# Eleven up units of an MLP by seven half-size products instead of eight

## Chip, cores and metric

The kernel runs on one core of a Trainium2 chip. The metric is the device time of one execution in microseconds (us); a change is judged by medians of runs. All arithmetic is on float32 data.

## What is computed

The reference is a transformer block of width 1024 on 512 rows, followed by a second stack of two layers (pooling, attention, gated convolution FFNs). The change concerns the MLP of the first block alone:

```
m = rms_norm(h, mlp_norm[i])                       # h: 512 x 1024
h = h + jnp.square(jax.nn.relu(m @ w_mlp_up[i])) @ w_mlp_down[i]   # up: 1024 x 4096, down: 4096 x 1024
```

## The kernel before

Activations are held transposed: 8 blocks of 128 channels on the partitions by 512 rows. A product of two float32 matrices is made of three TensorE products, because each operand is split into a high part (rounded to the multiplier's float32r format) and a low part (the rest): high x high, high x low, low x high. AH and AL are the parts of the activations, WH and WL those of the weights, HH and HL those of the squared hidden values.

The weights are cut into units of 128 x 2048 floats, listed in PLAN. A unit `up i` gives the hidden tiles m = 2i and 2i+1, each 128 hidden channels by 512 rows: 2 tiles x 8 channel blocks x 3 = 48 matmuls of 128x128 by 128x512 into one PSUM bank a tile. A unit `down i` is as large; groups of four down units consume eight hidden tiles and add their result to X. The order in the MLP is up 0 to 4, down 0 to 3, up 5 to 8, down 4 to 7, up 9 to 12, down 8 to 11, up 13 to 15, down 12 to 15. Before, the order is written in `mlp_order` and all engines walk through the same list.

Each engine runs its own program in order and waits on semaphores. SP loads a unit into one of two RAW buffers once the low part of the unit two before is made (`load`, L2457). ACT copies RAW to the high part in one of three WH slots (`split`, L1287), when PE is done with what the slot held; DVE subtracts to get the low part WL (`split`, L1677). A hidden tile goes: DVE takes relu and scale from PSUM (L2156, mark "up"), ACT squares (L1516) and rounds (L1519, mark "hh"), DVE makes HL (L2158, mark "hl"). DVE adds a down result to X (L1707). PE's triples of a tile are at L585 to L587, and those with the weights moving (the pooling stage: 256 columns) at L591 to L593. Six PSUM banks and a seventh are taken in a ring; the eighth holds norm sums. POOL issues a few DMAs during the MLP (`ev`, `pe_x`).

Of the kernel before, what the change touches and what calls it, by code (L numbers as in the profile page):

```python
# [15 lines left out]
P = 128  # L16
# [154 lines left out]
def memory(nc, ctx):  # L171
# [14 lines left out]
    k.WH = [a.tile(f"WH{i}", [P, UE], R) for i in range(NW)]  # L186
    wl_at = a.at
    k.WL = [a.tile(f"WL{i}", [P, UE], R) for i in range(NW)]
    k.rb = a.tile("rb", [P, S])
    k.sq = [a.tile(f"sq{i}", [P, S]) for i in range(2)]  # L190
    dg_at = a.at
    k.dg = a.tile("dg", [P, 4, P])
# [64 lines left out]
    k.pH = a.tile("pH", [P, 2, S], R)  # L257
    k.pL = a.tile("pL", [P, 2, S], R)
    k.pj = a.tile("pj", [P, 8, S])
    rel_at = a.at  # L260
    k.rel = a.tile("rel", [16, 513])
    k.ev = a.tile("ev", [16, 640])
# [64 lines left out]
    return (k.WH[j][:, 0:n].rearrange("p (k n) -> p k n", k=kc), k.WL[j][:, 0:n].rearrange("p (k n) -> p k n", k=kc))  # L327


def arrived(k, name):  # L330
    return k.arrived[name], 16


def mlp_order():

    for g in range(5):
        for i in range(4 * g, 4 * g + 1) if g < 4 else ():
            yield from up_order(i)
        if g > 0:
            for i in range(4):  # L340
                yield "split", UNIT["down", 4 * (g - 1) + i] + 2
                yield "down", g - 1, 2 * i
                yield "down", g - 1, 2 * i + 1
        for i in range(4 * g + 1, 4 * g + 4) if g < 4 else ():
            yield from up_order(i)
# [221 lines left out]
def tensor_program(k, e):  # L567
# [426 lines left out]
    def down(name, g, n, base, kc, m):  # L994

        u = UNIT[name, 4 * g + m // 2]
        a, l = split_view(k, u, kc)
        b = next_bank(7)
        cols = slice(m % 2 * P, m % 2 * P + P)
        w.wait_ge(WLO(u), *free[b])  # L1000
        for c in range(kc):
            s = (base + c) % NH
            w.wait_ge(DVE("hl", name, base + c))
            t = triple(bank[b][:, :], a[:, c, cols], l[:, c, cols], k.HH[s][:, :], k.HL[s][:, :], c == 0, c == kc - 1)
        t.then_inc(*in_bank(b, "res", n, m))
        free[b] = [DVE("x", n, m)]
        if m % 2:
            MM.also("unit", u)

    opened = {}  # L1010
    for step, *x in mlp_order():
        if step == "open":
            w.wait_ge(WLO(UNIT["up", 0]))
            bs = [next_bank(7), next_bank(7)]
            w.wait_ge(*free[bs[0]], *free[bs[1]])
            for c in TILES[:7]:
                w.wait_ge(DVE("al", 1, c))
                for i in range(2):
                    product(UNIT["up", 0], 8, i, bs[i], ks=[c], ends=(TILES[0], TILES[7]))
        elif step == "close":  # L1020
            m, = x
            w.wait_ge(DVE("al", 1, TILES[7]))
            product(UNIT["up", 0], 8, m, bs[m], ks=TILES[7:], ends=(TILES[0], TILES[7])).then_inc(*in_bank(bs[m], "up", m))
            free[bs[m]] = [DVE("up", m)]
            MM.also("unit", UNIT["up", 0])
        elif step == "tile":
            m, = x
            b = next_bank(7)
            w.wait_ge(WLO(UNIT["up", m // 2]), *free[b])
            product(UNIT["up", m // 2], 8, m % 2, b).then_inc(*in_bank(b, "up", m))  # L1030
            free[b] = [DVE("up", m)]
            MM.also("unit", UNIT["up", m // 2])
        elif step == "sums":
            norm_sums(1, DVE("acc", 1, 7))
        elif step == "spread":
            norm_spread(1)
        elif step == "down":
            g, m = x
            down("down", g, 2 + g, 8 * g, 8, m)

# [232 lines left out]
def scalar_program(k, e):  # L1273
# [4 lines left out]
    def split(u, *also):  # L1278

        if u >= len(PLAN):  # L1280
            return
        n = PLAN[u][2]
        w.wait_ge(loaded(k, u), *also)
        before = [v for v in range(u) if SLOT_OF[v] == SLOT_OF[u]]
        if before:
            w.wait_ge(MM("unit", before[-1]))
# [207 lines left out]

    w.wait_ge(arrived(k, "pe"))
    e.activation(k.pH[:, :, :], k.pe_x[:, :, :], AF.Copy).then_inc(*ACT.mark("pH"))

    def free_high(name, m, n0, group_of):  # L1500

        if m >= NH:
# [2 lines left out]
    for step, *x in mlp_order():  # L1505
        if step == "split":
            split(*x)
        elif step == "spread":
            spread_rows(1)
        elif step == "rest":  # L1510
            m, = x
            i = m % 2
            w.wait_ge(DVE("up", m))
            if m > 1:
                w.wait_ge(DVE("hl", "down", m - 2))
            e.activation(t2s[i][:, :], k.t1s[i][:, 0:S], AF.Square).then_inc(*ACT.mark("usq", m))  # L1516
            w.wait_ge(ACT("usq", m))
            free_high("down", m, 2, lambda m: m // 8)
            e.activation(k.HH[m % NH][:, :], t2s[i][:, :], AF.Copy).then_inc(*ACT.mark("hh", "down", m))  # L1519
        elif step == "down":  # L1520
# [143 lines left out]
def vector_program(k, e):  # L1664
# [462 lines left out]

    w.wait_ge(ACT("pH"))  # L2130
    e.tensor_tensor(k.pL[:, :, :], k.pe_x[:, :, :], k.pH[:, :, :].bitcast(F), SUB).then_inc(*DVE.mark("pL"))
# [5 lines left out]
    def parts(n, gcol, c, used):  # L2137

        w.wait_ge(DVE("x", k.x_of[n], c), used)
        e.tensor_scalar(AH[:, c, :], X[:, c, :], gain(gcol, c), None, MUL).then_inc(*DVE.mark("ah", n, c))  # L2140
        low_part(n, gcol, c, DVE("ah", n, c))

    for step, *x in mlp_order():
        if step == "split":
            split(*x)
        elif step == "sums":
            mean_square(1)
        elif step == "spread":
            spread_rows(1)
        elif step == "rest":  # L2150
            m, = x
            i, s = m % 2, m % NH
            w.wait_ge(MM("up", m), ACT("rb", 1))
            if m > 1:
                w.wait_ge(ACT("usq", m - 2))
            e.scalar_tensor_tensor(k.t1s[i][:, 0:S], bank[where["up", m]][:, :], 0.0, rb[:, :], MAX, MUL).then_inc(*DVE.mark("up", m))  # L2156
            w.wait_ge(ACT("hh", "down", m))
            e.tensor_tensor(k.HL[s][:, :], t2s[i][:, :], k.HH[s][:, :].bitcast(F), SUB).then_inc(*DVE.mark("hl", "down", m))  # L2158
        elif step == "down":
# [199 lines left out]
def pool_program(k, e):  # L2359
# [40 lines left out]


    w.wait_ge(DVE("al", 1, 3), MM("res", 16, 3))
    e.dma_start(k.pe_x[:, :, :], k.PT).then_inc(k.arrived["pe"], 16)
    e.dma_start(k.rel[:, :], k.REL).then_inc(k.arrived["rel"], 16)
    root(1)
    w.wait_ge(DVE("ev"))
    for i in range(16):
        w.wait_ge(MM("up", 2 * i))
        e.dma_start(k.EV.ap()[i:i + 1], k.ev[i:i + 1, None, :].to_broadcast([1, 64, 640])).then_inc(k.arrived["ev"], 16)
    w.wait_ge((k.arrived["ev"], 256))  # L2410
    e.dma_start(k.BC[:, :, :, :], k.BND).then_inc(k.arrived["band"], 16)
    root(2)
# [229 lines left out]
```

## Time and profile before

| | |
|---|---|
| median of 3 runs | 1646.34 us (1645.31 to 1647.6) |
| span of the profiled execution | 1644.3 us |
| PE busy | 1638.7 us, 8084 matmuls |
| PE weight loads busy | 1336.2 us, 8084 |
| DVE busy | 939.2 us, 1385 instructions |
| ACT busy | 615.9 us, 828 instructions |

The profiled execution's own time is its span; outside the span lie some 2 us up to the median of the runs. The page's engines: PE is TensorE, DVE is VectorE, ACT is ScalarE, SP and POOL issue DMAs. Matmuls overlap by their latencies, so their pace is read from starts, not from lengths.

### The profile page before, as it was taken

To read this page: it belongs to the slowest core of one execution; us is meant where nothing else is said; L and a number is where in the kernel's file an instruction comes from. 1 tells how busy PE (TensorE), PEld (TensorE's weight loads), DVE (VectorE), ACT (ScalarE), POOL (GpSimd) and SP (SyncE) were. 2 spreads that over 40 slices of the span, in tenths; PEclk is the share of its full clock that TensorE was granted. 3 is DMA by queue.
4 is the path that set the end of the run, shared out by engine and by line. 5 is a ranking of instruction groups with operands and counts; after the bars stand their busy time and mean duration, and the time that the engine had idled before them with its cause. 6 is when DMAs were issued, how large, how long until landed. Compare 5 with 4: busy or idle time off the path is not lost.

```text
span 1644.3 us, 19097 instructions
## 1 busy us (share of the span) xinstructions
PE 1638.7 (100%) x8084; PEld 1336.2 (81%) x8084; DVE 939.2 (57%) x1385; ACT 615.9 (37%) x828; POOL 84.6 (5%) x80
## 2 busy tenths in 40 slices
PE   9999999999999999999999999999999999999999
PEld 7877878888888888888888888877777888888887
DVE  6797665444333547577466457555655576366353
ACT  5576344322332346433222223355565333122121
POOL 1300000000000000000000000311201100000000
PEclk9999999999999999999999999999999999999999
DMA  5310227454454421223322223323221223222311
GB/s 187 116 36 27 103 93 128 120 89 130 87 111 85 135 88 52 77 103 107 124 83 96 103 83 100 123 78 101 77 76 52 77 103 104 102 102 94 110 59 71
DMA packets 28054, 155.94 MB, mean 95 GB/s; under 512 B 3712, under 2 KB 5392, under 8 KB 12096
## 3 DMA queue, kind: packets, MB, share of 16 engines
q1 hardware_dynamic: 26352, 149.75, 25.6%
q0 software_dynamic: 1328, 4.86, 5.0%
q8 instruction: 64, 1.05, 0.3%
q14 instruction: 22, 0.18, 0.0%
q10 hardware_dynamic: 288, 0.10, 0.0%
HBM read 149.98 MB, written 4.72 MB: 94 GB/s over the span
## 4 chain that ended last, share of the span: by engine, by line
PE 98%; ACT 1%; DVE 1%; POOL 0%; DMA 0%; issue 0%; SPq 0%; DVEq 0%
PE bank L585 26%; PE bank L587 26%; PE bank L586 26%; PE bank L591 3%; PE bank L593 3%; PE bank L592 3%; PE bank L1216 1%; PE bank L840 1%; PE bank L1226 1%; PE bank L1242 1%; PE bank L825 1%; PE bank L865 1%; PE bank L850 1%; PE bank L769 0%; PE bank L1102 0%; PE bank L1204 0%
## 5 line engine op out<-in xcount | busy, mean ns | idle before, releaser
L585 PE MATMUL bank<-AH,WH 128*128 128x512 f32 (+1 forms) x1150 | 451.4, 393 | 0.2 <-DVE X L1707 0.2
L587 PE MATMUL bank<-AH,WL 128*128 128x512 f32 (+1 forms) x1150 | 447.8, 389 | 0.0
L586 PE MATMUL bank<-AL,WH 128*128 128x512 f32 (+1 forms) x1150 | 447.6, 389 | 0.0
L1677 DVE TENSOR_TENSOR WL<-RAW,WH 128x2048 fp32r<-128x2048 f32 (+1 forms) x133 | 298.5, 2247 | 190.7 <-ACT WH L1287 190.7
L1287 ACT ACTIVATE WH<-RAW 128x2048 fp32r<-128x2048 f32 (+1 forms) x133 | 248.3, 1871 | 260.1 <-PE bank L587 240.3
L585 PEld LDWEIGHTS bank<-AH,WH 128*128 128x128 f32 (+1 forms) x1150 | 215.5, 187 | 48.0 <-issue 2.6
L587 PEld LDWEIGHTS bank<-AH,WL 128*128 128x128 f32 (+1 forms) x1150 | 215.5, 187 | 45.8
L586 PEld LDWEIGHTS bank<-AL,WH 128*128 128x128 f32 (+1 forms) x1150 | 215.6, 187 | 45.6 <-issue 1.0
L585 PE MATMUL bank<-HH,WH 128*128 128x512 f32 x608 | 239.6, 394 | 0.0
L587 PE MATMUL bank<-HH,WL 128*128 128x512 f32 x608 | 238.4, 392 | 0.0
L586 PE MATMUL bank<-HL,WH 128*128 128x512 f32 x608 | 236.0, 388 | 0.0
L1707 DVE TENSOR_TENSOR X<-X,bank 128x512 f32<-128x512 f32 x111 | 76.0, 685 | 192.2 <-PE bank L587 192.1
L587 PEld LDWEIGHTS bank<-HH,WL 128*128 128x128 f32 x608 | 114.1, 188 | 26.8
L586 PEld LDWEIGHTS bank<-HL,WH 128*128 128x128 f32 x608 | 114.1, 188 | 25.5
L585 PEld LDWEIGHTS bank<-HH,WH 128*128 128x128 f32 x608 | 114.3, 188 | 22.8
L1596 ACT ACTIVATE t2s<-t2s,par 128x512 f32<-128x512 f32 x44 | 31.9, 724 | 186.8 <-DVE t2s L2261 186.8
L591 PE MATMUL bank<-WH,AH 128*128 128x512 f32 x224 | 90.0, 402 | 0.0
L593 PE MATMUL bank<-WH,AL 128*128 128x512 f32 x224 | 87.5, 391 | 0.0
L592 PE MATMUL bank<-WL,AH 128*128 128x512 f32 x224 | 87.3, 390 | 0.0
L1601 ACT ACTIVATE HH<-cvs 128x512 fp32r<-128x512 f32 x44 | 27.8, 632 | 126.0 <-DVE cvs L2267 126.0
L1516 ACT ACTIVATE t2s<-t1s 128x512 f32<-128x512 f32 x32 | 20.2, 632 | 97.4 <-DVE t1s L2156 97.4
L1294 ACT ACTIVATE sq<-X 128x512 f32<-128x512 f32 x49 | 30.9, 630 | 65.6 <-DVE X L1707 61.6
(306 smaller groups left out, 1732.9 us busy)
## 6 DMA issues: line engine op xcount, KB each, us to landing
RAW<-in_W SPq DMA_DIRECT2D x124, 1024.0 KB, 4.8
RAW<-in_W SPq DMA_DIRECT2D x9, 768.0 KB, 4.1
X<-in_XT SPq DMA_DIRECT2D x16, 256.0 KB, 5.5
ev_scratch<-ev POOLq DMA_DIRECT2D x16, 160.0 KB, 7.5
Gb<-ev_scratch SPq DMA_DIRECT2D x16, 128.0 KB, 2.9
Gb<-ev_scratch SPq DMA_DIRECT2D x16, 112.0 KB, 2.7
out<-X SPq DMA_DIRECT2D x7, 256.0 KB, 2.0
RAW<-in_W SPq DMA_DIRECT2D x2, 512.0 KB, 5.4
```

Of the source, the lines that this page charges most:

```text
L585: e.matmul(o, a, h, start=first, stop=False)
L586: e.matmul(o, a, l, start=False, stop=False)
L587: return e.matmul(o, c, h, start=False, stop=last)
L591: e.matmul(o, h, a, start=first, stop=False)
L592: e.matmul(o, h, c, start=False, stop=False)
L593: return e.matmul(o, l, a, start=False, stop=last)
L1287: e.activation(k.WH[SLOT_OF[u]][:, 0:n], k.RAW[RAW_OF[u]][:, 0:n], AF.Copy).then_inc(*WHI.mark(u))
L1294: e.activation(k.acc if j == 0 else sq[(j - 1) % 2][:, :], src, AF.Square).then_inc(*ACT.mark("sqr", n, j))
L1596: e.activation(t2s[i][:, :], t2s[i][:, :], AF.Silu, bias=par[:, PC_CB + 22 * l + m:PC_CB + 22 * l + m + 1]).then_inc(*ACT.mark("silu", l, m))
L1601: e.activation(k.HH[m % NH][:, :], k.cvs[i][:, :], AF.Copy).then_inc(*ACT.mark("hh", name, m))
L1677: e.tensor_tensor(k.WL[j][:, 0:n], k.RAW[RAW_OF[u]][:, 0:n], k.WH[j][:, 0:n].bitcast(F), SUB).then_inc(*WLO.mark(u))
L1707: e.tensor_tensor(X[:, m, :], X[:, m, :], src, ADD).then_inc(*DVE.mark("x", n, m))
```

## The change

Up units 5 to 15 (`FAST`) are computed as a 2 x 2 block product with seven products of half-size blocks in place of eight: a, c, b, f, d, g, e (`FORMS`), each 4 channel blocks x 3 parts = 12 matmuls of 128x128 by 128x256, that is 84 matmuls a unit in place of 48. The inputs are sums of blocks. Of the activations these are made once, during down 0 to 3 (`shapes`, tiles TH and TL). Of the weights, three sums S1, S2, S3 are made for each fast unit in `stage`, and S4 is written over a block of RAW (`added`); four plus three quarter pieces are then split. WH and WL become rings of 12 quarter pieces; a fast unit takes 7, a plain one 4. The outputs need seven additions of blocks (`first_row`, `second_row`, `y`). The order inside a turn (one unit's time on PE) is written out in `turn_order`. The ACT and DVE work of hidden tiles moves into the steps "one", "two" and "low". The load of `pe_x` and its split move from before the MLP to down 13. The diff, cut:

```diff
+FIRST_FAST = 5
+FAST = {UNIT["up", i] for i in range(FIRST_FAST, 16)}
+FORMS = "acbfdge"
+def turn_of(u):
+    held = max((name[1] for name in held_until(u, 0, 4)), default=-1)
+    return min(max(held + 1, u - 2), u - 1)
+def turn_order(u):
+    _, i, _ = PLAN[u]
+    fast = u in FAST
+    if u - 1 in FAST:
+        yield "two", u - 1
+    for v in (u + 1, u + 2):
+        if turn_of(v) == u:
+            if v not in FAST:
+                yield "split", v
+            else:
+                if turn_of(v) == v - 2:
+                    yield "add", v
+                yield "raw", v
+    if fast:
+        yield "mid", u
+    if u - 1 in FAST:
+        yield "low", 2 * PLAN[u - 1][1] + 1
+    if u + 1 in FAST:
+        yield "stage", u + 1
+    if u + 2 in FAST and turn_of(u + 2) == u + 1:
+        yield "add", u + 2
+    if fast:
+        yield "one", u
+        yield "low", 2 * i
+    else:
+        if i < 3:
+            for c in ((0, 1), (2,), (3,))[i]:
+                yield "shapes", c
+        yield "down", i // 4, 2 * (i % 4)
+        yield "down", i // 4, 2 * (i % 4) + 1
+        if i == 13:
+            yield "pe",
 PE
+    def fast_products(u):            # step "mid"
+        bs = [next_bank(7) for _ in range(3)]
+        w.wait_ge(WLO(u), *free[bs[0]])
+        w.wait_ge(*(DVE("tl", c) for c in range(4)))
+        form_product(u, "a", bank[bs[0]])
+        w.wait_ge(WLO("stage", u))
+        form_product(u, "c", bank[bs[0]])
...
+        form_product(u, "g", bank[bs[2]])
+        w.wait_ge(DVE("y", u))
+        form_product(u, "e", bank[bs[0]])
 ACT
+        elif step == "raw":
+            w.wait_ge(loaded(k, u), DVE("s4", u), *(MM(*name) for name in held_until(u, 0, 4)))
+            for h, _, cols in ring_views(k, u, 0, 4):
+                t = e.activation(h, k.RAW[RAW_OF[u]][:, cols], AF.Copy)
+        elif step == "stage":
+            w.wait_ge(DVE("s2", u), *(MM(*name) for name in held_until(u, 4, 3)))
+        elif step == "mid":
+            w.wait_ge(MM("form", u, "c"), DVE("z", before) if before else DVE("t4", 3))
+            e.activation(k.G[:, 0:256], bank[k.where["fast", u][0]][:, 0:256], AF.Copy).then_inc(*ACT.mark("q1", u))
+        elif step in ("one", "two"):
+            w.wait_ge(DVE("up", m), DVE("hl", "down", m - 2))
+            e.activation(t2s[i][:, :], k.t1s[i][:, 0:S], AF.Square).then_inc(*ACT.mark("usq", m))
+            e.activation(k.HH[m % NH][:, :], t2s[i][:, :], AF.Copy).then_inc(*ACT.mark("hh", "down", m))
 DVE
+    def added(u):                    # step "add"
+        w.wait_ge(loaded(k, u), MM("spread", 1), *([WLO("stage", before)] if before else []))
+        e.tensor_tensor(k.stage[:, 0:2, :], raw[:, 0:4:3, :], raw[:, 2:3, :].to_broadcast([P, 2, QUARTER]), ADD)   # s1
+        e.tensor_tensor(k.stage[:, 2, :], raw[:, 0, :], k.stage[:, 1, :], ADD)      # waits s1, marks s2
+        e.tensor_tensor(raw[:, 2, :], raw[:, 1, :], k.stage[:, 2, :], ADD)          # waits s2, marks s4
+    def first_row(u):                # step "one"
+        w.wait_ge(MM("form", u, "g"), DVE("y", u))
+        e.tensor_tensor(k.G[:, 256:512], k.YZ[:, 0, :], bank[b[2]][:, 256:512], ADD)    # t
+        e.tensor_tensor(k.t1s[0][:, 0:S], k.G[:, :], bank[b[1]][:, :], ADD)             # row, waits t
+        e.scalar_tensor_tensor(k.t1s[0][:, 0:S], k.t1s[0][:, 0:S], 0.0, rb[:, :], MAX, MUL)   # up, waits row
+    def second_row(u):               # step "two": z (waits form e), row, up, likewise
+        elif step == "raw":
+            w.wait_ge(WHI(u))        # then WL = RAW - WH, 2048 columns, marks WLO(u)
+        elif step == "stage":
+            w.wait_ge(WHI("stage", u))   # then 1536 columns, marks WLO("stage", u)
+        elif step == "mid":
+            w.wait_ge(ACT("q1", u))
+            e.tensor_tensor(k.YZ[:, 0, :], k.G[:, 0:256], bank[...][:, 256:512], ADD).then_inc(*DVE.mark("y", u))
+        elif step == "low":
+            w.wait_ge(ACT("hh", "down", m))
+            e.tensor_tensor(k.HL[m % NH][:, :], t2s[m % 2][:, :], k.HH[m % NH][:, :].bitcast(F), SUB)
```

In a turn of a fast unit u between two others the list of steps is thus: two u-1, raw u+1, mid u, low (odd tile of u-1), stage u+1, add u+2, one u, low (even tile of u). Every engine takes its part of each step in this order.

## Rows read from the trace of the kernel before

**Rows 1.** The page, its first line and the chain that ended last, by engine.
```profile
span 1644.3 us, 19097 instructions
...
PE 98%; ACT 1%; DVE 1%; POOL 0%; DMA 0%; issue 0%; SPq 0%; DVEq 0%
```

**Rows 2.** Three stretches of the MLP: us, busy time (instructions) of each engine.
```profile
432.00:465.00 33.00, 33.00 (x148) 27.31 (x147) 14.91 (x15) 12.75 (x16) 1.51 (x3) 1.00 0.67 97
465.00:476.00 11.00, 11.00 (x50) 9.04 (x49) 4.96 (x5) 3.64 (x4) 0.00 (x0) 1.00 0.57 112
476.00:520.00 44.00, 44.00 (x194) 36.14 (x193) 14.80 (x13) 8.94 (x6) 0.50 (x1) 1.00 0.29 111
```

**Rows 3.** Timeline of PE, products of 512 columns: start, length (us).
```profile
344.82 0.39 PE L586 MATMUL bank<-AL,WH 128*128 128x512 f32 x1
...
351.85 0.39 PE L587 MATMUL bank<-AH,WL 128*128 128x512 f32 x1
```

**Rows 4.** Timeline of PE, products of 256 columns, in two stretches.
```profile
645.20 0.28 PE L591 MATMUL bank<-WH,HH 128*128 128x256 f32 x1
...
652.15 0.28 PE L593 MATMUL bank<-WH,HL 128*128 128x256 f32 x1
...
654.08 0.28 PE L591 MATMUL bank<-WH,HH 128*128 128x256 f32 x1
...
657.71 0.28 PE L593 MATMUL bank<-WH,HL 128*128 128x256 f32 x1
```

**Rows 5.** Weight loads of the 256-column products, grouped: busy us, mean ns.
```profile
L591 PEld LDWEIGHTS bank<-WH,HH 128*128 128x128 f32 x32 | 6.0, 188 | 0.0
```

**Rows 6.** Timeline of DVE, one up unit of the MLP.
```profile
450.47 2.29 DVE L1677 TENSOR_TENSOR WL<-RAW,WH 128x2048 fp32r<-128x2048 f32 x1 [1.12 <-ACT WH L1287]
452.68 0.68 DVE L2156 SCALAR_TENSOR_TENSOR t1s<-bank,rb 128x512 f32<-128x512 f32 x1
454.73 0.69 DVE L2158 TENSOR_TENSOR HL<-t2s,HH 128x512 fp32r<-128x512 f32 x1 [1.36 <-ACT HH L1519]
457.49 0.69 DVE L2156 SCALAR_TENSOR_TENSOR t1s<-bank,rb 128x512 f32<-128x512 f32 x1 [2.07 <-PE bank L587]
459.54 0.69 DVE L2158 TENSOR_TENSOR HL<-t2s,HH 128x512 fp32r<-128x512 f32 x1 [1.36 <-ACT HH L1519]
461.35 2.29 DVE L1677 TENSOR_TENSOR WL<-RAW,WH 128x2048 fp32r<-128x2048 f32 x1 [1.12 <-ACT WH L1287]
```

**Rows 7.** Timeline of DVE, two neighbouring down units.
```profile
317.30 2.29 DVE L1677 TENSOR_TENSOR WL<-RAW,WH 128x2048 fp32r<-128x2048 f32 x1 [1.32 <-ACT WH L1287]
...
328.29 2.29 DVE L1677 TENSOR_TENSOR WL<-RAW,WH 128x2048 fp32r<-128x2048 f32 x1 [1.32 <-ACT WH L1287]
```

**Rows 8.** Timeline of ACT, same up unit.
```profile
447.33 0.63 ACT L1516 ACTIVATE t2s<-t1s 128x512 f32<-128x512 f32 x1 [3.52 <-DVE t1s L2156]
448.00 0.63 ACT L1519 ACTIVATE HH<-t2s 128x512 fp32r<-128x512 f32 x1
448.53 1.91 ACT L1287 ACTIVATE WH<-RAW 128x2048 fp32r<-128x2048 f32 x1
```

**Rows 9.** DVE by line and shape, 240 to 264 us: busy us, mean ns.
```profile
L2131 DVE TENSOR_TENSOR pL<-pe_x,pH 128x1024 fp32r<-128x1024 f32 x1 | 1.2, 1225 | 2.0 <-ACT pH L1498 2.0
...
L1689 DVE TENSOR_SCALAR m<-bank 128x4 f32<-128x4 f32 x1 | 0.1, 143 | 0.0
```

**Rows 10.** Timeline of DVE, an addition and what reads its result.
```profile
551.09 0.68 DVE L1707 TENSOR_TENSOR X<-X,bank 128x512 f32<-128x512 f32 x1
551.80 0.49 DVE L2140 TENSOR_SCALAR AH<-X,par 128x512 fp32r<-128x512 f32 x1
```

**Rows 11.** The page, loads of weights: KB each, us from issue to landing.
```profile
RAW<-in_W SPq DMA_DIRECT2D x124, 1024.0 KB, 4.8
```

**Rows 12.** Timeline of PE, start of the execution.
```profile
1.06 4.21 PE L658 MATMUL bank<-rb 128*128 128x128 f32 x18 [1.06 <-DVE rb L1729]
...
7.80 0.40 PE L585 MATMUL bank<-AH,WH 128*64 128x512 f32 x1
```

More of the change, by code:

```diff
@@ L334, in mlp_order @@
 def mlp_order():
[L336 to L345, printed above, removed]
+    for i in range(FIRST_FAST):
+        yield from up_order(i)
+    for u in range(UNIT["down", 0], UNIT["down", 15] + 1):
+        yield from turn_order(u)
+def turn_order(u):
[22 more added lines that the diff above has]
+        yield "low", 2 * i
+    else:
+        if i < 3:
[5 more added lines that the diff above has]
+            yield "pe",
 def up_order(i):
@@ L1008, in down, with form_product @@
             MM.also("unit", u)
+    left, right = slice(0, 256), slice(256, 512)
+    moving = {"a": (AH, AL, 0, left), "b": (AH, AL, 4, left), "f": (AH, AL, 4, right), "g": (AH, AL, 0, right)}
+    half_bank = {"a": (0, left), "c": (0, right), "b": (1, left), "f": (1, right), "g": (2, left), "d": (2, right), "e": (0, right)}
+    def form_product(u, x, b):
+        place = places(u)[FORM_OF[x]] * QUARTER
+        n, cols = half_bank[x]
+        for c in range(4):
+            a, l = (z[:, place + c * P:place + c * P + P] for z in (k.WHR, k.WLR))
+            if x in moving:
+                zh, zl, c0, half = moving[x]
+                h, lo = zh[:, c0 + c, half], zl[:, c0 + c, half]
+            else:
+                h, lo = (z[:, c, "dce".index(x), :] for z in (k.TH, k.TL))
+            e.matmul(b[:, cols], a, h, start=c == 0 and x in "abd", stop=False, skip_group_check=True)
+            e.matmul(b[:, cols], a, lo, start=False, stop=False, skip_group_check=True)
+            t = e.matmul(b[:, cols], l, h, start=False, stop=c == 3, skip_group_check=True)
+        t.then_inc(*MM.mark("form", u, x))
+    def fast_products(u):
+        m = 2 * PLAN[u][1]
+        bs = [next_bank(7) for _ in range(3)]
+        k.where["fast", u] = bs
+        w.wait_ge(WLO(u), *free[bs[0]])
[3 more added lines that the diff above has]
+        form_product(u, "c", bank[bs[0]])
+        w.wait_ge(*free[bs[1]])
+        form_product(u, "b", bank[bs[1]])
+        form_product(u, "f", bank[bs[1]])
+        w.wait_ge(*free[bs[2]])
+        form_product(u, "d", bank[bs[2]])
+        form_product(u, "g", bank[bs[2]])
+        w.wait_ge(DVE("y", u))
+        form_product(u, "e", bank[bs[0]])
+        for name in (("up", m), ("up", m + 1), ("unit", u)):
+            MM.also(*name)
+        free[bs[0]], free[bs[1]], free[bs[2]] = [DVE("z", u)], [DVE("row", m)], [DVE("row", m + 1)]
     opened = {}
@@ new lines, in added @@
+    def added(u):
+        raw = k.RAW[RAW_OF[u]][:, :].rearrange("p (c n) -> p c n", c=4)
+        before = max((v for v in FAST if v < u), default=0)
+        w.wait_ge(loaded(k, u), MM("spread", 1), *([WLO("stage", before)] if before else []))
+        e.tensor_tensor(k.stage[:, 0:2, :], raw[:, 0:4:3, :], raw[:, 2:3, :].to_broadcast([P, 2, QUARTER]), ADD).then_inc(
+            *DVE.mark("s1", u))
+        w.wait_ge(DVE("s1", u))
+        e.tensor_tensor(k.stage[:, 2, :], raw[:, 0, :], k.stage[:, 1, :], ADD).then_inc(*DVE.mark("s2", u))
+        w.wait_ge(DVE("s2", u))
+        e.tensor_tensor(raw[:, 2, :], raw[:, 1, :], k.stage[:, 2, :], ADD).then_inc(*DVE.mark("s4", u))
@@ new lines, in first_row @@
+    def first_row(u):
+        m, b = 2 * PLAN[u][1], where["fast", u]
+        w.wait_ge(MM("form", u, "g"), DVE("y", u))
+        e.tensor_tensor(k.G[:, 256:512], k.YZ[:, 0, :], bank[b[2]][:, 256:512], ADD).then_inc(*DVE.mark("t", u))
+        w.wait_ge(DVE("t", u), ACT("usq", m - 2))
+        e.tensor_tensor(k.t1s[0][:, 0:S], k.G[:, :], bank[b[1]][:, :], ADD).then_inc(*DVE.mark("row", m))
+        w.wait_ge(DVE("row", m))
+        e.scalar_tensor_tensor(k.t1s[0][:, 0:S], k.t1s[0][:, 0:S], 0.0, rb[:, :], MAX, MUL).then_inc(*DVE.mark("up", m))
@@ L2158, in vector_program @@
             e.tensor_tensor(k.HL[s][:, :], t2s[i][:, :], k.HH[s][:, :].bitcast(F), SUB).then_inc(*DVE.mark("hl", "down", m))
+        elif step == "shapes":
+            shapes(*x)
+        elif step == "add":
+            added(*x)
+        elif step == "raw":
+            u, = x
+            w.wait_ge(WHI(u))
+            for h, l, cols in ring_views(k, u, 0, 4):
+                t = e.tensor_tensor(l, k.RAW[RAW_OF[u]][:, cols], h.bitcast(F), SUB)
+            t.then_inc(*WLO.mark(u))
+        elif step == "stage":
+            u, = x
+            w.wait_ge(WHI("stage", u))
+            for h, l, cols in ring_views(k, u, 4, 3):
+                t = e.tensor_tensor(l, k.stage[:, :, :].rearrange("p i n -> p (i n)")[:, cols], h.bitcast(F), SUB)
+            t.then_inc(*WLO.mark("stage", u))
+        elif step == "mid":
+            u, = x
+            w.wait_ge(ACT("q1", u))
+            e.tensor_tensor(k.YZ[:, 0, :], k.G[:, 0:256], bank[where["fast", u][0]][:, 256:512], ADD).then_inc(*DVE.mark("y", u))
+        elif step == "one":
+            first_row(*x)
+        elif step == "two":
+            second_row(*x)
+        elif step == "low":
+            m, = x
+            w.wait_ge(ACT("hh", "down", m))
+            e.tensor_tensor(k.HL[m % NH][:, :], t2s[m % 2][:, :], k.HH[m % NH][:, :].bitcast(F), SUB).then_inc(*DVE.mark("hl", "down", m))
+        elif step == "pe":
+            w.wait_ge(ACT("pH"))
+            e.tensor_tensor(k.pL[:, :, :], k.pe_x[:, :, :], k.pH[:, :, :].bitcast(F), SUB).then_inc(*DVE.mark("pL"))
         elif step == "down":
```

117 lines of the change are left out of this document (108 added, 9 removed).

## Prediction

> **What bounds the kernel now.** I read the chain that ended last first: it lies on PE for 98% of a span of 1644.3 us [rows 1]. So every matmul removed from the MLP is worth its pace, if what feeds PE keeps up. Next, the stretches by engine: in 33 us of three up units DVE is busy 14.9 and ACT 12.8, in 44 us of four down units 14.8 and 8.9 [rows 2]. The reader is to see that both have about half of their time free, and that this is a mean over a simple pattern. Last, the timelines, for paces and hand-overs. The pace of PE is the distance of starts: 512-column products start 7.03 us apart over 31 intervals, 0.2268 us each [rows 3]. An up unit (48) is 10.88 us, which is also the distance of DVE's splits there, 450.47 to 461.35 [rows 6]; a down unit takes 10.99 [rows 7].
>
> **What PE gains.** Products of 256 columns stand in the trace: 59 intervals of 0.1178 us and 32 of 0.1134 [rows 4]. The second is half of 0.2268 to the digit. I take 0.1134: a fast unit is 84 x 0.1134 = 9.53 us in place of 10.88, 11 units give 11 x 1.35 = -14.9 us (by 0.1178: 9.90 and -10.8). A bound from above is the weight load, 188 ns long [rows 5]; loads of neighbouring products overlap in rows 4, or these could not start 0.113 apart.
>
> The Trainium skill (TensorE: Matmul & The Clock Gate, Back-to-back issue gap) gives 81 ns for 128 columns and 131 for 512 in a sustained stream, so half the columns would cost much more than half. By a line between its figures (an estimate) 256 columns take about 98 ns and a fast unit 8.2 us against 6.3 for 48 full ones, 1.9 us more; rows 3 and 4 do not agree with either figure, and the measured paces decide.
>
> **What the change adds on DVE and ACT.** DVE lengths: 0.69 us for 512 columns, 1.225 for 1024, 2.29 for 2048 [rows 6, 9], a straight line of 0.267 us a 256 columns. So 256 columns take 0.42 and 1536 take 1.76. The 256-column price is not in the trace; its bounds are 0.14 (4 columns) and 0.69 [rows 6, 9], and I take the line because three points lie on it. The next instruction starts 0.08 before the end of one that it does not depend on (450.47 to 452.68 for 2.29), and 0.03 after the end of one that it does [rows 6, 10]. ACT: 0.63 for 512, 1.91 for 2048 [rows 8], 0.03 more to hand over, 0.54 to the next independent one.
>
> Now one whole turn between two fast units, from one step `y` to the next, in DVE's order, which is fixed:
> - y 0.34, low 0.61, low parts of the stage 1.68, its end 0.11: 2.7.
> - add: s1 on 1024 columns 1.25, s2 0.72, s4 0.61: 2.6.
> - first row: t 0.45, row 0.72, up 0.72: 1.9. Then DVE can only wait: the next step, low, needs ACT's square 0.66 and rounding 0.66: 1.3. low itself 0.6.
> - second row: 1.9. Then `raw` waits on ACT, whose list has square 0.66, rounding 0.54 and only then the high parts of 2048 columns 1.94: 3.1. Low parts of raw 2.2. Then y.
>
> Sum 16.4 us (16.7 where a unit wraps the ring and its split is two instructions), 10.9 of it busy. PE has 9.53 us of work in it. The last product of a unit, e, waits for y, and the next unit's products stand behind e in PE's queue; so PE stops before e, 6.9 to 7.1 us a full turn. A turn without add (the fourth unit of a group; the third of the last) is 13.8: stop 4.2 to 4.3. In a group's first fast unit y starts 4.35 us after its first product (c at 2.7, ACT, raw), while e is due at 8.2: no stop. Its loop to the second unit is 17.2 (the stage waits for product b), of which 9.5 is work and 3.4 the slack just named: 4.3. The same additions for the last group, where one add lies elsewhere, give 4.1.
>
> Stops before e: 4.3 + 7.1 + 4.2, 4.3 + 6.9 + 4.2, 4.1 + 4.3 = 39.4 us.
>
> **One more wait, at down 12.** Its first accumulation needs hidden tile 31 in its eighth block. From y of unit up 15 DVE and ACT need: y and low 0.95, first row 1.9, ACT 1.3, low 0.6, second row 1.9, ACT square, rounding and the split of down 13 3.1, then DVE's splits of down 13 and down 14, 4.4, which stand ahead of low(31) in the list, and low 0.7: 15.0. PE: 0.46 to y's end, e 1.36, 21 products 4.8: 6.6. Stop 8.4. In the other groups the first down unit reads tiles finished long before: nothing.
>
> **Edits that I cost at nothing.** shapes: a column block is 8 DVE instructions, 3.9 us, and about 1 of waiting on ACT, four times 20 us, within 44 us of down units in which DVE is busy 14.8 [rows 2]; with two adds and a stage (2.6 twice and 1.8) that is 42. The last TL is made 5.5 us before up 5 needs it, the stage of up 5 4 us before product c. Without this cover up 5 starts later by what is missing. Additions to X wait longer, but seven banks give them more than two down units. Loads: a RAW buffer is freed with the low parts of raw and filled 4.8 us later [rows 11], while its reader is at least 5 us behind. The load of `pe_x` goes behind the last `ev` issue on POOL's queue and is read a down unit or more later. The split of `pe_x` was off PE's path before, so moving it gives nothing.
>
> **The clock.** At the start of the execution 18 small products take 4.21 us, and the first product of 0.40 us stands at 7.80 [rows 12]; the products between are longer. After a pause, then, PE may work at the lower of its two levels for up to 6.7 us, which costs half of that, 3.4. Before e this is paid out of the stops themselves (9.5 + 3.4 is less than 13.8). Only after the 8.4 us stop nothing covers it: 0 to 3.4, I take 2.
>
> **Sum.** 1644.3 - 14.9 + 39.4 + 8.4 + 2 = 1679.2 against the profiled span; the median of the runs is 2.0 above that span: **1681 us**.
>
> **Rivals.**
> 1. VectorE keeps up. For: it is half idle [rows 2]. Against: 10.9 us of its own work a full turn against 9.5. The mechanism would be that the steps between y and y overlap the hand-overs, so that only the work counts. Then there are two stops of 1.4 and the last of perhaps 6: -14.9 + 9 gives 1640; with none at all, 1631. It decides from where the stops together fall below 14.9 us, 1.7 each over nine in place of 5.3. Chance 0.05, a little of it within 0.2% of before.
> 2. Half-size products do not cost half: PE would wait for weight loads. At 0.188 us [rows 5] a fast unit is 15.8 us, 11 x 4.9 = +54, and of the stops only the last, 7, is left: 1707. Against: rows 4. Chance 0.02. The skill's rule on issue gaps, above, points this way.
> 3. The clock stays low through the runs of fast units, since PE pauses in each. At 0.2268 us for 256 columns a unit is 19.0 us, longer than VectorE's loop: 11 x 8.1 + 7 = +96: 1742 at the end, and anything between for a part. For: every turn has a pause of 4 to 7 us, which the trace of before never has behind its start. Against: the clock came up within 6.7 us of work, and a unit is 9.5. Chance 0.08. The Trainium skill (TensorE: Matmul & The Clock Gate, Why this matters for your kernels) warns that idle gaps between bursts send the clock back to the lower level; no run so far shows this within a kernel.
>
> The forecast has 0.85.
>
> **Range.** The 256-column price, three a loop, at 0.14 or 0.69 moves nine loops by 0.8 each, 8 us either way; hand-overs of 0.02 to 0.08 in place of 0.03 move the total by -3 to +8; PE's pace hardly moves it, since the fast runs go by VectorE; the clock 0 to 3.4, or more in rival 3. Together 1667 to 1700. What a measurement of this kernel can tell from no change is about 0.2%, 3 us: faster 0.05, same 0.02, slower 0.93.
>
> **What would show it.** Starts of y 16 to 17.5 us apart inside a group and 13.8 at its end; a PE timeline with idle time before product e released by DVE YZ, 40 us in sum, and 8 us before the last block of down 12's first tile, released by HL; DVE near 11 of 16.5 us busy; the ACT copy of RAW waiting on nothing but its place in the queue. 256-column products at 0.113 to 0.118 apart. I am wrong if e does not wait, if idle time stands elsewhere (before product a or c: splits late; before the first down product: loads), or if the pace inside a burst is 0.227.

## The result and the profile after

The median is 1686.03 us (1684.21 to 1688.71, 4 runs) against 1646.03 us (1645.31 to 1647.6) before: ratio 1.0236, 95% interval 1.0223 to 1.025, slower by 40 us. The forecast was 1681 us, in a range of 1667 to 1700. The profiled execution spans 1683.7 us, 39.4 us more than before. Its page, first line and chain by engine, to be read against [rows 1]:

```profile
span 1683.7 us, 20082 instructions
...
PE 70%; DVE 7%; ACT 3%; issue 1%; POOL 0%; DVEq 0%; ACTq 0%
```

The chain was followed back from the end to 320 us only, so its shares add to 81% of the span. VectorE and ScalarE, which had 1% each before, now have 10% together. Two stretches of the MLP, the first group of fast units and the down units behind it, columns as in [rows 2] and then the granted clock:

```profile
338.00:393.00 55.00, 45.82 (x337) 45.16 (x337) 39.65 (x50) 20.28 (x25) 1.51 (x3) 0.88 0.46 70
393.00:437.80 44.80, 44.80 (x194) 36.31 (x193) 24.10 (x25) 11.46 (x9) 0.50 (x1) 1.00 0.41 118
```

In 55 us of four fast units VectorE is busy 39.7 us, three quarters of the time, and PE 45.8; the granted clock is 0.88 on average. In the down units VectorE has time left. What PE waited for in the MLP (us in total, times, longest):

```profile
PE bank L1134 <- DVE YZ L2415: 23.3, 8, 6.1
PE bank L694 <- DVE HL L2423: 7.9, 1, 7.9
```

L1134 is the first product of each triple of a fast unit, and its waits stand before e; the one at L694 stands before the first down product that reads hidden tile 31. These are the two waits of the forecast, 31.2 us together. VectorE between the y of unit up 6 and that of up 7, to be read against [rows 6]:

```profile
360.74 0.41 DVE L2415 TENSOR_TENSOR YZ<-G,bank 128x256 f32<-128x256 f32 x1
361.07 0.68 DVE L2423 TENSOR_TENSOR HL<-t2s,HH 128x512 fp32r<-128x512 f32 x1
361.68 1.75 DVE L2410 TENSOR_TENSOR WLR<-stage,WHR 128x1536 fp32r<-128x1536 f32 x1
363.53 1.23 DVE L2352 TENSOR_TENSOR stage<-RAW 128x1024 f32<-128x1024 f32 x1
364.79 0.69 DVE L2355 TENSOR_TENSOR stage<-RAW,stage 128x512 f32<-128x512 f32 x1
365.52 0.69 DVE L2357 TENSOR_TENSOR RAW<-RAW,stage 128x512 f32<-128x512 f32 x1
366.13 0.42 DVE L2363 TENSOR_TENSOR G<-YZ,bank 128x256 f32<-128x256 f32 x1
366.58 0.69 DVE L2365 TENSOR_TENSOR t1s<-G,bank 128x512 f32<-128x512 f32 x1
367.30 0.69 DVE L2367 SCALAR_TENSOR_TENSOR t1s<-t1s,rb 128x512 f32<-128x512 f32 x1
369.35 0.69 DVE L2423 TENSOR_TENSOR HL<-t2s,HH 128x512 fp32r<-128x512 f32 x1 [1.36 <-ACT HH L1699]
369.96 0.41 DVE L2373 TENSOR_TENSOR YZ<-G,bank 128x256 f32<-128x256 f32 x1
370.41 0.69 DVE L2375 TENSOR_TENSOR t1s<-YZ,bank 128x512 f32<-128x512 f32 x1
371.13 0.69 DVE L2378 SCALAR_TENSOR_TENSOR t1s<-t1s,rb 128x512 f32<-128x512 f32 x1
375.07 2.36 DVE L2404 TENSOR_TENSOR WLR<-RAW,WHR 128x1536 fp32r<-128x1536 f32 x2 [3.25 <-ACT WHR L1679]
377.35 0.41 DVE L2415 TENSOR_TENSOR YZ<-G,bank 128x256 f32<-128x256 f32 x1
```

From y to y are 16.61 us (forecast 16.4 to 16.7). L2410 is the stage's low part, L2352 to L2357 the add, L2363 to L2367 the first row, L2423 the low parts of hidden tiles, L2373 to L2378 the second row, L2404 raw. Two gaps are to be seen: 1.36 us before the low part at 369.35, and 3.25 before the split at 375.07. What ScalarE did in the second, to be read against [rows 8]:

```profile
371.86 0.63 ACT L1696 ACTIVATE t2s<-t1s 128x512 f32<-128x512 f32 x1 [2.53 <-DVE t1s L2378]
372.52 0.63 ACT L1699 ACTIVATE HH<-t2s 128x512 fp32r<-128x512 f32 x1
373.06 1.99 ACT L1679 ACTIVATE WHR<-RAW 128x1536 fp32r<-128x1536 f32 x2
```

ScalarE makes the square, the rounding, and only then the high parts that VectorE waits for. y starts 15.92, 16.61 and 13.66 us apart in the first group, 17.28, 16.44 and 13.66 in the second, 16.95 and 13.74 in the third. PE behind the first stop, and the same products later in the unit:

```profile
361.21 0.58 PE L1134 MATMUL bank<-TH,WHR 128*128 128x256 f32 x1 [4.29 <-DVE YZ L2415]
361.59 0.41 PE L1135 MATMUL bank<-TL,WHR 128*128 128x256 f32 x1
361.81 0.41 PE L1136 MATMUL bank<-TH,WLR 128*128 128x256 f32 x1
...
373.28 0.28 PE L1134 MATMUL bank<-AH,WHR 128*128 128x256 f32 x1
373.40 0.28 PE L1135 MATMUL bank<-AL,WHR 128*128 128x256 f32 x1
373.52 0.28 PE L1136 MATMUL bank<-AH,WLR 128*128 128x256 f32 x1
```

Behind the stop products of 256 columns start 0.21 us apart, later 0.12; the granted clock (the column before the last two) in the two stretches:

```profile
361.20:366.50 5.30, 5.29 (x25) 5.29 (x26) 5.13 (x6) 0.00 (x0) 0.50 (x1) 0.51 1.01 216
366.50:373.60 7.10, 7.10 (x61) 7.09 (x60) 3.82 (x7) 2.98 (x5) 0.00 (x0) 1.00 0.37 12
```

That is 1.2 and 2.4 GHz. The down products behind the first group, first shown and last of the group, 190 intervals apart:

```profile
393.25 0.40 PE L695 MATMUL bank<-HL,WH 128*128 128x512 f32 x1
...
437.59 0.40 PE L696 MATMUL bank<-HH,WL 128*128 128x512 f32 x1
```

They are 0.2333 us apart; those of down 0 to 3 stay at 0.2290. Down 12 begins at 0.2334 and runs at 0.2292 behind its stop.

Where the 39.4 us lie, by starts of products on PE (a group is measured from the last product of the down units ahead to the first behind; down 0 to 3 take 43.7 us in both and are left out):

| | before | after | more | forecast |
|---|---|---|---|---|
| up to the first down product | 293.1 | 294.1 | +1.0 | 0 |
| up 5 to 8 | 43.8 | 55.2 | +11.4 | +10.2 |
| up 9 to 12 | 43.8 | 54.1 | +10.3 | +10.0 |
| up 13 to 15 | 32.9 | 37.5 | +4.6 | +4.4 |
| down 4 to 7, 8 to 11 | 43.7 each | 44.6 each | +1.7 | 0 |
| down 12 to 15 | 43.7 | 54.3 | +10.5 | +10.4 |
| all that follows | 1055.5 | 1055.5 | 0 | 0 |

The forecast column is the prediction's stops less 1.35 us for each fast unit. The first row is not of the change. It goes with a fall of the clock at 192 us, ahead of the MLP, that one profile has and the other has not. The same stretch before and after:

```profile
192.00:196.00 4.00, 4.00 (x22) 3.39 (x23) 0.84 (x2) 3.03 (x3) 1.64 (x1) 1.00 0.00 0
```

```profile
192.00:196.00 4.00, 4.00 (x12) 3.16 (x12) 1.41 (x2) 2.46 (x3) 1.64 (x1) 0.57 0.00 0
```

Six of the eleven profiles here have these 3.4 us at a granted clock of 0.50, and in them the first down product stands at 294.1 to 294.7; in the five without, that of the kernel before among them, it stands at 292.5 to 293.1. PE had not stopped ahead of it.

### The profile page after: what moved, and what is told of

Same layout as the page of the kernel before. It is cut to its first block, busy times and chain, and to the rows that moved or that the text cites. A ratio compares the mean times of both kernels' runs of the same rounds, so it can differ in the third digit from the quotient of the medians.

```text
span 1683.7 us, 20082 instructions
## 1 busy us (share of the span) xinstructions
PE 1647.1 (98%) x8480; PEld 1360.8 (81%) x8480; DVE 1027.0 (61%) x1525; ACT 639.3 (38%) x867; POOL 84.6 (5%) x80
## 4 chain that ended last, share of the span: by engine, by line
PE 70%; DVE 7%; ACT 3%; issue 1%; POOL 0%; DVEq 0%; ACTq 0%
PE bank L694 19%; PE bank L696 19%; PE bank L695 19%; PE bank L700 3%; PE bank L702 2%; PE bank L701 2%; PE bank L1369 1%; PE bank L1379 1%; PE bank L1395 1%; DVE WLR L2404 1%; DVE WLR L2410 1%; ACT WHR L1679 1%; DVE WL L1860 1%; ACT WH L1438 1%; ACT t2s L1696 1%
## 5 line engine op out<-in xcount | busy, mean ns | idle before, releaser
L1860 DVE TENSOR_TENSOR WL<-RAW,WH 128x2048 fp32r<-128x2048 f32 (+2 forms) x122 | 273.0, 2243 | 187.2 <-ACT WH L1438 187.2
L694 PE MATMUL bank<-AH,WH 128*128 128x512 f32 (+1 forms) x974 | 383.1, 393 | 0.2
L696 PE MATMUL bank<-AH,WL 128*128 128x512 f32 (+1 forms) x974 | 379.3, 389 | 0.0
L695 PE MATMUL bank<-AL,WH 128*128 128x512 f32 (+1 forms) x974 | 379.2, 389 | 0.0
L1438 ACT ACTIVATE WH<-RAW 128x2048 fp32r<-128x2048 f32 (+2 forms) x122 | 226.9, 1866 | 170.2 <-PE bank L696 139.9
L694 PE MATMUL bank<-HH,WH 128*128 128x512 f32 x608 | 240.9, 396 | 7.9 <-DVE HL L2423 7.9
L694 PEld LDWEIGHTS bank<-AH,WH 128*128 128x128 f32 (+1 forms) x974 | 182.5, 187 | 41.7 <-issue 2.6
L696 PEld LDWEIGHTS bank<-AH,WL 128*128 128x128 f32 (+1 forms) x974 | 182.5, 187 | 38.9
L695 PEld LDWEIGHTS bank<-AL,WH 128*128 128x128 f32 (+1 forms) x974 | 182.6, 187 | 38.6 <-issue 1.0
L694 PEld LDWEIGHTS bank<-HH,WH 128*128 128x128 f32 x608 | 115.0, 189 | 32.3 <-DVE HL L2423 8.3
L1779 ACT ACTIVATE t2s<-t2s,par 128x512 f32<-128x512 f32 x44 | 31.9, 724 | 186.8 <-DVE t2s L2529 186.8
L1134 PE MATMUL bank<-TH,WHR 128*128 128x256 f32 x132 | 41.0, 310 | 23.3 <-DVE YZ L2415 23.3
```

The costliest lines, as they stand in the source:

```text
L694: e.matmul(o, a, h, start=first, stop=False)
L695: e.matmul(o, a, l, start=False, stop=False)
L696: return e.matmul(o, c, h, start=False, stop=last)
L1134: e.matmul(b[:, cols], a, h, start=c == 0 and x in "abd", stop=False, skip_group_check=True)
L1779: e.activation(t2s[i][:, :], t2s[i][:, :], AF.Silu, bias=par[:, PC_CB + 22 * l + m:PC_CB + 22 * l + m + 1]).then_inc(*ACT.mark("silu", l, m))
L1860: e.tensor_tensor(k.WL[j][:, 0:n], k.RAW[RAW_OF[u]][:, 0:n], k.WH[j][:, 0:n].bitcast(F), SUB).then_inc(*WLO.mark(u))
```

## The experiments

Each is the kernel after the change with an edit, timed beside the kernel before. The last three build on one another. Diffs are cut at the marks.

**ScalarE's copy first.** The turn's list gets another order for ScalarE alone:

```diff
+def scalar_turn(u):
+
+    steps = list(turn_order(u))
+    if u in FAST and u - 1 in FAST:
+        first = [s for s in steps if s[0] in ("raw", "split")]
+        steps = first + [s for s in steps if s not in first]
+    return steps
...
+    for step, *x in mlp_order(scalar_turn):
```

> The kernel after the change with one thing moved: in a turn of a fast unit that follows a fast unit, ScalarE copies the high parts of the next unit's weights (step raw, or the split of a down unit) before the square and the rounding of the last hidden tile (step two), not behind them. No instruction is added or left out. Theory A (VectorE's in-order loop from y to y sets the pace, and 3.1 us of it is waiting on ScalarE's list): each loop between two fast units gets about 3.2 us shorter; starts of y come 13.4 us apart where they were 16.6 and about 10.5 where they were 13.7; PE's waits before product e fall from 23 us to about 7 to 9; the wait of 7.9 us at down 12 stays; in all 26 us less, some 2 to 4 more because the clock falls less often: median 1656 to 1661. Theory B (the seven products and VectorE's amount of work, not the order, cost the time): ScalarE was not busy, VectorE's busy time is unchanged, so less than 5 us is gained: 1681 to 1686. Theory C (the low clock costs the time on its own): as B.

Measured: 1659.2 us (ratio 1.0076, 1.0061 to 1.0091), 27 us less than the 1686.0 after the change, by one move. VectorE in the turn that took 16.61 us, and PE's waits:

```profile
356.51 0.41 DVE L2424 TENSOR_TENSOR YZ<-G,bank 128x256 f32<-128x256 f32 x1
...
366.90 0.69 DVE L2387 SCALAR_TENSOR_TENSOR t1s<-t1s,rb 128x512 f32<-128x512 f32 x1
367.51 2.35 DVE L2413 TENSOR_TENSOR WLR<-RAW,WHR 128x1536 fp32r<-128x1536 f32 x2
369.78 0.41 DVE L2424 TENSOR_TENSOR YZ<-G,bank 128x256 f32<-128x256 f32 x1
```

```profile
PE bank L703 <- DVE HL L2432: 7.9, 1, 7.9
PE bank L1143 <- DVE YZ L2424: 7.3, 4, 2.9
```

The split at 367.51 follows the second row without a gap, y starts 13.27 us after the last one, and PE waits 7.3 us before e where it waited 23.3. The wait at down 12 (L703) is still 7.9. The stops shrink by 16 us and the groups by 26, eight loops of 3.3: most of the rest is products that no longer run at the low clock, which fell once here in place of four times in the groups. Theory A holds; B and C, which left the order no weight, fall.

**The last low part first.** VectorE's list in the down unit behind a group:

```diff
+    if u not in FAST and u - 1 in FAST:
+        low = [s for s in steps if s[0] == "low"]
+        steps = steps[:1] + low + [s for s in steps[1:] if s not in low]
```

> The kernel after the change with one thing moved on VectorE: in the first down unit behind a group of fast units, the low part of the last hidden tile is made right behind the second row, before the two splits of down units. Nothing is left out. Theory A: the wait of 7.9 us before the eighth block of down 12 falls by the two splits less one rounding hand-over, to about 2 us, and with so short a stop the clock does not fall behind it (24 slow products less, 2.4 us): 1677 to 1680. Rival: the low part was not what held it (the wait then stays above 6 us, or turns into one before the next down unit, whose split now comes later): 1683 to 1687.

Measured: 1677.04 us (ratio 1.0181, 1.0165 to 1.0196), 9 us less. The wait fell from 7.9 to 1.7 us, and no slow product stands behind it, as theory A said.

**Filler on PE.** Products into an idle bank before e, and 34 of 512 columns before the eighth block of down 12 (cut):

```diff
+        for n in range(FILL.get(m // 2, 0)):
+            e.matmul(bank[7][:, 0:256], k.TH[:, n % 4, 0, 0:P], k.TH[:, n % 4, 0, :], start=True, stop=True)
         w.wait_ge(DVE("y", u))
```

> The kernel after the change with filler work on TensorE: before product e of units 6, 7, 8, 10, 11, 12, 14, 15 there are 26 to 52 products of 256 columns into an otherwise unused bank, and 34 of 512 columns before the eighth block of down 12, in number about what fills the idle time measured there. The output is the same. The fillers keep the clock up. Theory A (stops are set by VectorE, the clock costs only what no stop covers): each group of fast units takes what it took in its undisturbed form: 54.0 us for the first (55.2 measured), 54.1 and 37.5 as before; down 12 to 15 take 2.4 us less, the product rows behind the stops are at 0.120 and not 0.2135; in all 2 to 4 us less: 1682 to 1684. Theory C (the fall of the clock is a large part of the 40 us): groups get shorter by 3 us or more each, 1675 or less. If the fillers are too many, groups get longer by the excess.

Measured: 1682.91 us (ratio 1.0217, 1.0202 to 1.0232), within the 1682 to 1684 of theory A; theory C falls. PE hardly waits any more:

```profile
PE bank L1138 <- DVE YZ L2421: 1.0, 1, 1.0
PE bank L695 <- DVE HL L2429: 0.2, 1, 0.2
```

The groups take 55.2, 54.1 and 37.5 us, to 0.1 us what they took with idle PE and a clock that fell. Down 12 to 15 take 52.0 in place of 54.3. So the clock cost 2.3 us, all of it behind the last stop (forecast 2); inside groups it was paid out of the stops. That the first group would come down to 54.0 was wrong: its 1.1 us over the second are not the clock's. They are VectorE's. In the first group y comes 6.8 us after the unit's first product, in the second 4.4. In down 3 the add of unit up 6 stands behind `shapes` and two additions to X and starts at 337.90, 0.1 us before the fast unit does; in down 7 that of up 10 starts 7.6 us before. No run leaves `shapes` out, so that it is the cause is read from the timeline and not shown by a run.

**The add twice.** Each of the three additions is done again behind itself:

```diff
+        e.tensor_tensor(k.stage[:, 0:2, :], raw[:, 0:4:3, :], raw[:, 2:3, :].to_broadcast([P, 2, QUARTER]), ADD).then_inc(*DVE.mark("s1a", u))
+        w.wait_ge(DVE("s1a", u))
...
```

> The kernel after the change with each of the three additions of weight blocks (step add) done twice, the second waiting for the first and writing the same values. The output is the same. Each add costs VectorE 2.7 us more. Theory A (VectorE's loop is the bound inside groups): the two loops of a group of four that hold an add and the one in the group of three get 2.7 us longer each, a little slack at up 5 is used up, and adds in the down units cost nothing or 1 to 2 us: 5 x 2.7 and up to 4 more, 13 to 17 us: 1699 to 1703. Theory B (PE's own work and clock set the time, VectorE has slack): less than 4 us: up to 1690.

Measured: 1705.29 us (ratio 1.0354, 1.0337 to 1.0372), 19 us more by the medians and 16.5 by the spans of the profiles (this one lacks the clock fall at 192 us), above the 13 to 17 and the 1703 expected. The five loops with an add are 2.7 us longer each (18.62, 19.32; 19.99, 19.15; 19.66), the others unchanged. The miss is in the first group, 66.1 us in place of 55.2: 5.4 from its two loops, and 5.4 because y of the first unit comes 12.2 us after the unit's first product in place of 6.8, behind the doubled adds in down 2 and down 3, 2.7 each. The theory that VectorE has slack falls; the cover in the down units is thinner than I had it.

**All waits back.** `e.wait_ge(*DVE("hl", name, base + c))` in place of `w.wait_ge(...)`, for the pace of 0.2333.

> The kernel after the change with TensorE's wait for a hidden tile's low part issued before every block of every down product of the MLP, also where an earlier wait has already passed it. The output is the same. Question: why do the down products behind fast units start 0.2333 us apart in the kernel after, where those of down 0 to 3 and all of before start 0.2290 apart (0.83 us more for each of three groups of 192). Theory W: in the kernel after, TensorE's waits for y have passed the later counts, so the waits between the triples are no longer issued, and the wait instruction in the stream is what makes the pace 0.2290: with it back the pace is 0.2290 in all groups, spans 2.5 us shorter. Theory S (the ring's places or the tiles' addresses): 0.2333 stays, nothing changes.

Measured: 1685.9 us, one run; the pace stays at 0.2333. Theory W falls; theory S is not shown by it.

**128 columns.** The operands and the output of each fast product are cut to their first 128 columns, so half of each product is left out (cut):

```diff
+        cols = slice(cols.start, cols.start + P)
...
+                half = slice(half.start, half.start + P)
...
+                h, lo = (z[:, c, "dce".index(x), 0:P] for z in (k.TH, k.TL))
```

> The kernel after the change with each of the 84 products of a fast unit on 128 columns in place of 256; it leaves out half of the columns. Question: why are the products 0.120 us apart and not 0.1134. Theory I (a cost of each product and weight load that doesn't depend on columns, such as the issue of the two instructions): the pace stays at 0.120. Theory K (columns and something on top): it falls, to 0.107 to 0.110, where the trace of before has 128-column products. The time inside groups is VectorE's either way: the groups stay at 55.2, 54.1 and 37.5 us within 1, the waits before e grow by what the products lose, up to 1 us a unit; only e itself and the first products of down units follow it: total 1683 to 1687.

Measured: 1704.4 us, one run. At full clock the pace is 0.112. A cost of 0.120 that doesn't depend on columns would have left 0.120, so theory I falls as it was put; the 0.107 to 0.110 of theory K isn't reached either. Products of one column stand at 0.112 in every kernel here; the trace of the kernel after has 16 such records, each with its own weight load:

```profile
190.25 1.95 PE L1041 MATMUL bank<-cst,sq 128*128 128x1 f32 x16
192.06 0.59 PE L694 MATMUL bank<-OM,WH 128*128 128x512 f32 x1
```

That is 1.81 us over 16, 0.113. So the pace is 0.112 with one column and with 128, and only the step from 0.112 to 0.120 comes with the second 128. Cutting the columns by half gains 7%. The total went the other way. Granted clock and PE of two stretches of the first group:

```profile
361.00:378.00 17.00, 16.75 (x79) 16.75 (x79) 12.08 (x17) 6.05 (x8) 0.50 (x1) 0.50 0.49 72
378.00:399.50 21.50, 21.50 (x103) 21.50 (x102) 11.21 (x15) 4.80 (x7) 0.50 (x1) 0.50 0.52 106
```

Behind the first stop the clock stays at 0.50 for the rest of the group and 4 us into the down products behind it, though PE is busy all the time, and products of 128 columns stand 0.213 us apart. A unit is then 17.9 us, longer than VectorE's loop, and the groups are 61.9, 60.5 and 42.4 us. My expectation had left the clock out.

**Reordered.** Both moves, and the low part of each even tile put off to the next turn, behind the second row (cut):

```diff
+    if u in FAST:
+        steps = [s for s in steps if s != ("low", 2 * PLAN[u][1])]
+    if u - 1 in FAST:
+        low = [("low", 2 * PLAN[u - 1][1])]
+        if u not in FAST:
+            low += [s for s in steps if s[0] == "low"]
+        steps = steps[:1] + low + [s for s in steps[1:] if s not in low]
```

> The kernel after the change in another order and with nothing else: the two moves tried alone before (ScalarE's copy of the next weights first; the last low part before the splits in the down unit behind a group), and the low part of each even hidden tile put off to the next turn, behind the second row, so that VectorE doesn't wait 1.4 us for ScalarE there. Theory A, by the same sums of VectorE's loop (16.6 less 3.3 less 1.4): starts of y 12 us apart in a full turn and 9.5 to 10.1, TensorE's own, elsewhere; waits before e 5 to 7 us in all, none at down 12, no fall of the clock. Groups 44, 43 and 31 us, down 12 to 15 44.6: median 1644 to 1649, the time of before within 0.2%. Theory B (what is left of the loss belongs to the work of the change and not to the order): above 1651.

Measured: 1647.78 us (ratio 1.0004, 0.9995 to 1.0013): the time of before. Waits before e:

```profile
PE bank L1156 <- DVE YZ L2437: 5.4, 4, 2.5
```

Loops of y are 12.1, 12.8 and 9.8 us in the first group, groups 45.3, 42.8 and 31.2, down 12 to 15 43.8. With the same instructions in another order the whole loss of 40 us is gone; theory B falls. Nothing is left of a gain either: the three groups together are 1.2 us shorter than in the kernel before, and the down products behind two of them take 1.7 us longer. The clock did fall once, for 3.4 us from 368.5, behind the stop of 2.7 us; theory A had none. Down 12 to 15 run at 0.2290 here, with nothing added.

**Reordered and filled.** To this, 4 to 21 filler products where a stop was left, and ahead of down 4, 8 and 12:

```diff
+        if name == "down" and g > 0 and m == 0:
+            e.matmul(bank[7][:, 0:1], k.ident, k.ones[:, 0:1], start=True, stop=True)
```

> The reordered kernel of the run before with two additions on TensorE, both into an unused bank, the output the same: 4 to 21 filler products of 256 columns before product e of the four units that still wait there, and one float32 product of one column at the head of the first down unit behind each group. The fillers: in the reordered kernel the clock fell behind the 2.7 us stop of unit 7 (13 slow products, 1.2 us over their pace) and nothing covers that any more, so the first group should go from 45.3 to 44 us; the others stay at 42.8 and 31.2. The single product: a guess that the pace of 0.2333 of the down products behind a group is a matter of how loads and products are interleaved there and would be shifted by a hiccup, to 0.2290 (0.8 us a group); the rival is that it stays. In all 1.3 us less, with the guess 3: median 1644.5 to 1647, at best 0.1% under the kernel before the change.

Measured: 1645.07 us (11 runs) against 1646.81: ratio 0.9988, 0.9979 to 0.9997. The first group is 44.1 us. The single products, and the first and the last but one of the 192 down products behind them:

```profile
382.06 0.28 PE L1133 MATMUL bank<-cst 128*128 128x1 f32 x2
382.20 0.47 PE L717 MATMUL bank<-HH,WH 128*128 128x512 f32 x1
...
425.78 0.39 PE L718 MATMUL bank<-HL,WH 128*128 128x512 f32 x1
```

That is 43.58 us over 190 intervals, 0.2294, and 0.2290 from the second product on; one matmul of float32 operands stands in the trace as two records. The same holds for down 8, so both groups of four down units that ran at 0.2333 in the reordered kernel now run at 0.2290: the guess held. Fillers alone, in the filler run above, had left them at 0.2333. This is the fastest version here and beats both kernels, by 0.12% over the one before the change, with an interval that ends at 0.03%.

**Single products in fast units too.** The same line before product a.

> The kernel of the run before with one more thing: the float32 product of one column, which brought the down products from 0.2333 back to 0.2294 us, also at the head of each of the eleven fast units. Question: is the pace of 0.120 in fast units, where the trace of before shows 0.1134 behind such products, the same effect. If so, the products of a fast unit go to 0.1134 to 0.118 and each unit takes 0.2 to 0.5 us less on TensorE; inside a group VectorE's loops of 12.1 to 12.8 us keep most of it, so 1 to 3 us less in all: 1642 to 1644.5. Rival: the pace is set by the stream of products of 256 columns and their weight loads; it stays at 0.120, and the median stays within 1 us of 1645.

Measured: 1645.84 us (ratio 0.9997, 0.9988 to 1.0006). The pace stays at 0.120 and each single product costs about 0.3 us: the groups are 44.6, 43.7 and 31.9 us. The rival holds in that the pace doesn't move; what sets it no run shows. The question itself rested on a pace that is not fixed. The stream of the pooling stage in which the trace of before had 0.1134 [rows 4] is the same in all kernels, single products ahead of it included, and here it runs at 0.1175:

```profile
653.78 0.28 PE L723 MATMUL bank<-WH,HH 128*128 128x256 f32 x1
...
657.54 0.28 PE L725 MATMUL bank<-WH,HL 128*128 128x256 f32 x1
```

## Why the prediction was right, and which terms were off

- **The loop from y to y** was right in kind and in size: 16.61 and 16.44 us for 16.4 to 16.7, 13.66 for 13.8, and 17.28 for the 17.2 behind a group's first unit (15.92 in the first group, where that unit's y was late). Moving ScalarE's copy took 3.3 us out of each full loop, doubling the add put 2.7 in. The 256-column additions took 0.41 us where I had 0.42. One figure beside the sum was wrong: the loop's busy time is not 10.9 us but 11.9, which is 16.4 less its two waits of 1.3 and 3.1; the profile has 11.7 of 16.65. No term of the forecast used it, but rival 1 did: its two stops of 1.4 should have been 2.4.
- **The wait at down 12** was right: 7.9 for 8.4 us (the terms given for VectorE add to 14.9, not 15.0), and it went with the move of one instruction.
- **PE's gain was mis-sized**, 11 x 1.35 us. I took 0.1134 for a product of 256 columns; the fast units run at 0.120, a unit is 10.08 us and 11 of them gain 8.8 us, not 14.9. It was even above the other row, 0.1178. That 0.1134 is half of 0.2268 was no reason to take it: the 34 intervals of that stretch, the same instructions in every kernel, are 0.1135 in six of the profiles and 0.1178 in the five others. The total did not feel it, since inside a group VectorE sets the length and a slower PE only shortens the stops. Together with the low clock (97 products 0.21 us apart in place of 0.12, 9 us) that is why the idle time before e is 23.3 us and not 39.4. A right total does not vouch for this term. Rival 2, which wanted 0.188, is refuted by the rows at 0.120.
- **The clock** fell, as rival 3 feared, but came back within 5 to 6 us of 256-column work, and the filler shows a cost of 2.3 us for the 2 I took. Rival 3's stretch of low clock through a whole group shows in the 128-column run, but not by its mechanism, a pause in each turn: there one stop was enough, and the clock stayed low with PE busy.
- **shapes at no cost** was wrong by 1.1 us. y of the first unit came 6.8 us after the unit's first product, not 4.35. That unit had the slack for it, which I had looked at; the add behind it and the second unit's y had not.
- **The down products at 0.2333** behind a group, 1.7 us, I had not seen.
- Rival 1, that VectorE keeps up, needed the hand-overs to go. Reordered they mostly do; a loop with an add in it is then 12.1 to 13.5 us, still above PE's 10.1, and the change gains and loses nothing.

The 4.4 us between forecast and span are thus 1.0 ahead of the MLP, with the clock fall at 192 us, 1.7 of pace, 1.1 of shapes and 0.6 of smaller terms.

## To carry to other kernels

An engine that is half idle on average can still set the pace: sum its work and its waits from one point of the loop to the same point, in its own order, and compare that with the time of the engine that you speed up. Look in that list for an instruction that waits on a second engine whose copy stands behind something nobody needs yet; here one such place cost 27 of 40 us. Before saving work on the busiest engine, ask whether the saving (0.8 us a unit) is larger than what is added elsewhere (VectorE is busy 39.7 us in the first group, where it was 19.3).

## What the runs showed of the hardware

- Products with a weight load each were 0.120 us apart at 256 columns in a long stream, 0.112 at 128, and 0.112 at one: below 256 columns little is gained. At a granted clock of 0.50 both 256 and 128 columns take 0.213 us. The Trainium skill (TensorE: Matmul & The Clock Gate, LDWEIGHTS) has a load of 128 columns at their number over 1.2 GHz, 107 ns, which is near the floor of 0.112 us at full clock. The trace's own record of such a load is longer, 0.19 us at full clock and 0.33 at 0.50, and neighbouring loads overlap; at the low clock pairs of 128 columns stand twice as far apart as 107 ns, which the section does not say.
- A stop of PE of about 4 us was followed by 5 to 6 us at a granted clock of 0.50 in some places and by none in others: the stop that ends at 460 us, 3.4 us long, has none behind it in the profile after and 5.5 us in that with the last low part first. A stop of 2.7 us was followed by a fall in the reordered kernel, and six of eleven profiles have one at 192 us with no stop ahead of it. With products of 128 columns the clock stayed at 0.50 for 38 us of an always busy PE, and it rose about 4 us after products of 512 columns had begun.
- Products of equal shape and tiles run at one of two paces: down products at 0.2290 or 0.2333 us, constant over 192 products where nothing comes between, and the 34 intervals of 256 columns in the pooling stage at 0.1135 or 0.1178. In both runs that had it, a float32 product of one column ahead of down 4 and of down 8 moved them from 0.2333 to 0.2290; it did nothing to the 0.120 of fast units, and in the last run the pooling stage ran at 0.1178 behind such products. It is not the only thing that does: behind the stop in down 12 the pace went from 0.2334 to 0.2292 in the profile after, and from 0.230 to 0.2332 in that with 128 columns. The cause stays open: wait instructions between products are not it, and places and addresses were the same in kernels that differ.
